# Mixer C's sample attention in pairs of sequences, squares summed by VectorE, and an unrolled layer loop, in a two-layer hybrid decoder step

## The reference

```
x = x + 1/2 * SwiGLU_1(rmsnorm(x))                 # 1024 -> 2048 -> 1024
h = rmsnorm(x);  z = h @ w_in                      # queries, keys, values, ... of three mixers
  A: dilated window attention, 3 groups of 4 heads # B: gated short convolution
  C: an indexer scores all keys, the best are kept, 8 query heads on 2 key/value heads attend to them
x = x + w_out( sum_i sigmoid(h @ w_gate)_i * (branch_i @ w_branch_i) )
x = x + 1/2 * SwiGLU_2(rmsnorm(x))
```

## Time and profile before

| what | us |
|---|---|
| median of three runs (lowest, highest) | 2748.9 (2746.89, 2760.05) |
| the profiled execution: its time, its span | 2747.25, 2745.7 |
| PE busy, share of the span | 2529.2 (92%) |
| DVE busy | 973.7 (35%) |
| ACT busy | 528.7 (19%) |
| POOL busy | 282.5 (10%) |
| DMA, mean over the span | 139 GB/s |

### The profile page before, as it was taken

The page is one execution under the profiler, slowest core; times in us unless marked ns, Lnnn a source line. Parts: engine busy times, 40 slices in busy tenths (PEclk is TensorE's granted clock), DMA queues, the critical chain, the costliest instruction groups (busy, mean ns, idle before and its releaser), DMA issues.

```text
span 2745.7 us, 33069 instructions
## 1 busy us (share of the span) xinstructions
PE 2529.2 (92%) x10482; PEld 1680.8 (61%) x10482; DVE 973.7 (35%) x1706; ACT 528.7 (19%) x1030; POOL 282.5 (10%) x532
## 2 busy tenths in 40 slices
PE   6997999998889899999989998999988898999998
PEld 4765567654447556667657664776544565676766
DVE  1001356754656542110010014667455664411000
ACT  2100221123221232111011003111323213311110
POOL 3430000000002120000243000000000102100000
PEclk9998999988999888999999999999899997789999
DMA  5475337373435341144446631573454443322342
GB/s 163 149 233 145 97 131 259 125 246 120 154 106 169 98 124 50 63 152 122 121 130 211 213 94 66 195 274 121 172 175 149 137 143 93 93 77 77 122 138 66
DMA packets 317953, 382.32 MB, mean 139 GB/s; under 512 B 23901, under 2 KB 300966, under 8 KB 316138
## 3 DMA queue, kind: packets, MB, share of 16 engines
q1 hardware_dynamic: 292290, 257.40, 30.3%
q0 software_dynamic: 19712, 118.79, 12.5%
q10 hardware_dynamic: 5800, 4.30, 0.5%
HBM read 374.80 MB, written 92.91 MB: 170 GB/s over the span
## 4 chain that ended last, share of the span: by engine, by line
PE 85%; DVE 5%; DMA 3%; issue 3%; ACT 3%; SPq 1%; DVEq 0%; ACTq 0%
PE ps L634 46%; PE ps L686 11%; PE ps L911 4%; PE ps L915 4%; PE ps L874 3%; PE ps L883 3%; PE ps L848 2%; PE ps L851 2%; PE ps L792 1%; DMA ring<-in_ffn_wd 1%; PE ps L901 1%; PE ps L728 1%; PE ps L823 1%; PE ps L738 1%; ACT pT L1024 1%
## 5 line engine op out<-in xcount | busy, mean ns | idle before, releaser
L634 PE MATMUL ps<-h,ring 128*128 128x320 f32 x3200 | 873.5, 436 | 21.5 <-DVE h L1300 17.8
L634 PEld LDWEIGHTS ps<-h,ring 128*128 128x128 f32 x3200 | 612.6, 192 | 279.0 <-DVE h L1300 11.4
L634 PE MATMUL ps<-area,ring 128*128 128x320 f32 x1280 | 355.1, 436 | 21.6 <-DMA ring<-in_ffn_wd 13.3
L686 PE MATMUL ps<-ring,h 128*128 128x256 f32 (+3 forms) x1440 | 321.3, 383 | 10.4 <-DVE h L1300 7.8
L634 PEld LDWEIGHTS ps<-area,ring 128*128 128x128 f32 x1280 | 244.4, 191 | 126.7 <-DMA ring<-in_ffn_wd 13.8
L686 PEld LDWEIGHTS ps<-ring,h 128*128 128x128 f32 (+1 forms) x1440 | 243.9, 178 | 82.8 <-issue 25.9
L1308 DVE TENSOR_TENSOR area<-silu,ps 128x320 f32 x64 | 31.2, 488 | 522.0 <-ACT silu L1049 522.0
L363 POOL DMA_DIRECT2D area<-in_cache_c_idx x256 | 137.0, 535 | 488.5 <-issue 473.6
L380 POOL DMA_DIRECT2D area<-in_cache_c_kv x176 | 98.5, 560 | 741.3 <-issue 741.3
L1024 ACT ACTIVATE kT<-ps 128x512 f32<-128x512 f32 (+3 forms) x248 | 125.9, 544 | 199.3 <-PE ps L851 118.8
L1315 DVE SCALAR_TENSOR_TENSOR x<-ps,x 128x320 f32<-128x320 f32 x48 | 23.6, 491 | 362.5 <-PE ps L634 362.5
(11 more groups left out here) (183 smaller groups left out, 2090.5 us busy)
## 6 DMA issues: line engine op xcount, KB each, us to landing
out_s_a_kv<-in_cache_a_kv POOLq DMA_DIRECT2D x64, 1020.0 KB, 9.1
ring<-in_w_in SPq DMA_DIRECT2D x80, 512.0 KB, 4.6
ring<-in_ffn_wg SPq DMA_DIRECT2D x64, 512.0 KB, 4.6
ring<-in_ffn_wu SPq DMA_DIRECT2D x64, 512.0 KB, 7.1
ring<-in_ffn_wd SPq DMA_DIRECT2D x64, 512.0 KB, 5.7
area<-in_cache_a_kv SPq DMA_DIRECT2D x32, 1024.0 KB, 6.5
ring<-in_w_gate SPq DMA_DIRECT2D x48, 512.0 KB, 4.5
area<-in_cache_c_kv POOLq DMA_DIRECT2D x176, 128.0 KB, 2.7
```

Of the source, the lines that this page charges most:

```text
L634: last = mm(bank(b, T), w[:, j, c0:c0 + P], rhs[:, j, :], start=(j == 0), stop=(j == k - 1))
L686: last = mm(dst, h3[:, k, t0:t0 + rows], w[:, k, :], start=(k == 0), stop=(k == KD - 1))
```

## The change

1. `sample_jobs` keeps kind "a" only. Mixer C gets functions of its own that take two sequences at a time, 4 pairs, with 64 score rows each, so all 128 PSUM partitions are used.
2. Keys are no longer turned by PE and copied by ACT: DVE turns the key half of a page buffer in place, in blocks of 32 x 32, in two instructions of 1024 columns per sequence. A score product then has 32 contraction rows and 32 output rows: one row quarter `q4` and one column group (sequence, kv head) of the array, 512 keys wide. There are 32 of them per pair, and their queries lie in `qR`, filled once per layer by 17 DVE copies (`c_queries`). The mask goes first, with four bf16 products of 512 columns and one of 64.
3. Maximum and exponential read PSUM directly (no DVE copy of the scores); the division by the sum moves behind the values, to a 128 x 128 piece. Probabilities are turned in 17 pieces of 128 x 128 for both sequences; values take 2 x 17 products with 64 output rows each, and the result is turned back by PE once per pair.
4. Four page buffers: the new one, with `kT`, `z`, `zt`, `y`, is the tensor `stage`. Sequences 0, 1 and 3 are loaded by POOL ahead of `chosenS`; 2, 4, 5, 6, 7 half by POOL and half by SP. 4 and 5 wait for the values of pair 0, 6 and 7 for those of pair 1.
5. The mean square: DVE adds the eight squares into the first one, PE makes one product per norm where it made eight.
6. `for l in range(DEPTH)` instead of the hardware loop, on all five engines; waits compare with constants.
7. Small memsets on DVE clear what the shared buffers have spoilt, since `stage`, `ab`, `uh`, `us`, `rot` now serve several purposes.

```diff
-SAMPLE_JOBS = 2 * NB
+SAMPLE_JOBS = NB
+PAIRS = NB // 2
-CBUFS = 3
+CBUFS = 4
+C_POOL = (16, 16, 8, 16, 8, 8, 8, 8)
+C_CHUNKS = ((0, 4), (4, 4), (8, 4), (12, 4), (16, 1))
...
-            with sp.Fori(0, DEPTH) as l:          (the same on every engine)
+            for l in range(DEPTH):
...
-                for b in range(CBUFS, NB):
-                    load_c_pages(sp, l, b, range(NPAGES // 2), c_in_sp)
+                sp.wait_ge(chosenS.sem, chosenS.at(l, 1))
+                alone(sp)
+                for b in (2, 4, 5, 6, 7):
+                    load_c_pages(sp, l, b, range(C_POOL[b], NPAGES), c_in_sp)
...
+                load_c_pages(pool, l, 0, range(NPAGES), c_in_pool)
+                load_c_pages(pool, l, 1, range(NPAGES), c_in_pool)
+                pool.wait_ge(k_out.sem, k_out.at(l, k_out.per_layer))
+                load_c_pages(pool, l, 3, range(NPAGES), c_in_pool)
                 pool.wait_ge(chosenS.sem, chosenS.at(l, 1))
+                for b in (2, 4, 5, 6, 7):
+                    load_c_pages(pool, l, b, range(C_POOL[b]), c_in_pool)
...
-            def mean_square(l, n, k):
-                pe.wait_ge(sq_ready.sem, sq_ready.at(l, (n - 1) * KD + k + 1))
-                ins = mm(bank(6, T), ones[:, :], squares[k], start=(k == 0), stop=(k == KD - 1))
+            def mean_square(l, n):
+                pe.wait_ge(sq_added.sem, sq_added.at(l, n * (KD - 1)))
+                mm(bank(6, T), ones[:, :], squares[0], start=True, stop=True).then_inc(ms_ready.sem, 1)
...
+                def c_scores(p):
+                    b0 = 2 * p
+                    pe.wait_ge(ck_turned.sem, ck_turned.at(l, b0 + 2))
+                    ...      # p == 0: wait for qR_ready; else: pe.wait_ge(cs_exp.sem, cs_exp.at(l, p))
+                    for q4 in range(4):
+                        mm(bank(q4), pick, hide, start=True, stop=False)
+                    mm(bank(4, NSAMP), pick, outS[:, PAST:KEYS], start=True, stop=False)
+                    for half in range(2):
+                        for s in range(2):
+                            for g in range(2):
+                                for q4 in range(4):
+                                    at, r0 = 2 * g + half, 64 * s + 32 * g
+                                    q = qR[q4 * 32:(q4 + 1) * 32, ((b0 + s) * 4 + at) * 32:((b0 + s) * 4 + at + 1) * 32]
+                                    k = cpages(b0 + s)[q4 * 32:(q4 + 1) * 32, :, at * 32:(at + 1) * 32]
+                                    mm(ps[r0:r0 + 32, q4 * 512:(q4 + 1) * 512], q, k, start=False, stop=(half == 1))
+                    ...      # four products with the 64 new keys
+                def c_turn(p, c):       # 4 (at last 1) transposes of 128 x 128 of probs into bank 5 + c % 2
+                def c_values(p, c):     # 8 (at last 2) products: 64 probabilities' columns x 128 values
+                def sample_c():
+                    c_scores(0); c_scores(1); c_out(0); c_out(1); c_back(1)
+                    c_scores(2); c_scores(3); c_out(2); c_out(3); c_back(3)
...
+                def sample_c():         # ACT, per pair p
+                        act.wait_ge(cs_max.sem, cs_max.at(l, p + 1))
+                        fn(probs ..., ps[:, 0:PAST] ..., ACT.Exp, ...)      # 128 x 2048
+                        fn(probs[:, PAST:KEYS], ps[:, PAST:KEYS], ACT.Exp, ...).then_inc(cs_exp.sem, 1)
+                        ...             # and a copy of each turned chunk
...
+                        if c >= 2:
+                            add_square(l, n + 1, c - 1)                     # DVE, in add_x
+                    add_square(l, n + 1, KD - 1)
...
+                def sample_c():         # DVE
+                    def keys_turn(b):
+                        ...             # waits for the pages of b
+                        for i in range(2):
+                            k = cpages(b)[:, 8 * i:8 * i + 8, 0:P]
+                            last = nc.vector.transpose(k, k)
+                    keys_turn(0); keys_turn(1); most(0); keys_turn(2); keys_turn(3); most(1); result(0); result(1)
+                    keys_turn(4); keys_turn(5); most(2); keys_turn(6); keys_turn(7); most(3); result(2); result(3)
```

More of the change, by code:

```diff
@@ L550, in _ @@
             pool.wait_ge(consts_in.sem, 48)
-            with pool.Fori(0, DEPTH) as l:
+            for l in range(DEPTH):
                 pool.wait_ge(x_ready.sem, x_ready.at(l, 1 - KD))
@@ L616, in _ @@
                 last.then_inc(turned_in.sem, 1)
-            for k in range(KD):
-                mean_square(0, 0, k)
-            with pe.Fori(0, DEPTH) as l:
+            mean_square(0, 0)
+            for l in range(DEPTH):
                 def arrived(q, i=0):
@@ L930, in sample_jobs @@
                     scores_of(0, 0)
-                    if kind == "a":
-                        with pe.Fori(0, NB // 2 - 1) as i:
-                            two(i)
-                    else:
-                        for i in range(NB // 2 - 1):
-                            two(i)
+                    with pe.Fori(0, NB // 2 - 1) as i:
+                        two(i)
                     scores_of(NB // 2 - 1, 1)
@@ new lines, in c_values @@
+                def c_values(p, c):
+                    n0, n_ = C_CHUNKS[c]
+                    pe.wait_ge(cs_pT.sem, cs_pT.at(l, p * len(C_CHUNKS) + c + 1))
+                    if c == 0 and p:
+                        pe.wait_ge(cs_done.sem, cs_done.at(l, p))
+                    for n in range(n0, n0 + n_):
+                        for s in range(2):
+                            v = cpages(2 * p + s)[:, n, P:256] if n < NPAGES else vc3[:, 2, :]
+                            last = mm(ps[64 * s:64 * s + 64, 7 * 512:7 * 512 + P], pTc[:, n * P + 64 * s:n * P + 64 * s + 64], v,
+                                      start=(n == 0), stop=(n == NPAGES))
+                    if c == len(C_CHUNKS) - 1:
+                        last.then_inc(cs_out.sem, 1)
@@ new lines, in c_back, with c_out @@
+                def c_back(p):
+                    pe.wait_ge(cs_rows.sem, cs_rows.at(l, p + 1))
+                    tr(bank(7, P, at=256), rowsC, ident).then_inc(cs_back.sem, 1)
+                def c_out(p):
+                    for c in range(len(C_CHUNKS) + 1):
+                        if c < len(C_CHUNKS):
+                            c_turn(p, c)
+                        if c == 1 and p % 2:
+                            c_back(p - 1)
+                        if c >= 1:
+                            c_values(p, c - 1)
@@ L1035, in _ @@
             squares_of_x(0, 0)
-            with act.Fori(0, DEPTH) as l:
+            for l in range(DEPTH):
                 def norm(n):
@@ L1423, in conv @@
                 def conv():
+                    step(nc.vector.memset(uh3[:, :, 0:2], 0.0))
                     for c in range(4):
@@ L1590, in _ @@
                 ffn(0)
+                for t in (z3, zt3, y3):
+                    last = nc.vector.memset(t[64:P, 2, :], 0.0)
+                step(last)
                 norm(1)
```

366 lines of the change are left out of this document (207 added, 159 removed).

## The result

The changed kernel takes 2580.9 us, the median of 4 runs (2574.6 to 2599.4), where the kernel before took 2754.5 us on the same chip: a ratio of 0.938, interval 0.932 to 0.944. The profiled execution went from 2747.25 to 2583.66 us, 163.6 us less.

What follows compares the result with a forecast made beforehand. PE was taken as the bound, with 85% of the chain, partly at its lower clock. Savings of 87.6 (sample stage), 15 (norms) and 6 (loop), 108.6 us, from 2747.25 gave 2639 us, range 2597 to 2710.

Steps and rivals of the forecast that it cites:

- The loop: Layer boundary: PE's 6.05 us with nothing to wait for disappears in straight code; 6 us saved once, 0 at worst.
- The sample stage: Mixer C's samples, summed step by step: 109.5 us against 152.3 and 154.3, saving 87.6 us over two layers.
- First keys: Start of mixer C's samples: DVE turns keys of sequences 0 and 1 while PE has nothing to do, 5.0 us.
- values of a pair: Mixer C's samples: 17 transposes and 34 products, half an overlap of the column halves at the high clock, 9.2 us.
- pages: Mixer C's samples: page loads of sequences 4 to 7, from end of pair 0's values to last page, 42.2 us.
- The 32 score products: Mixer C's samples, per pair: 4.5 us, between 8.0 with only row quarters overlapping and 2.0 with all 16 tiles.
- The new wait: Second half of mixer C's samples: PE waits for page issues, idle 15 us or more behind pair 1's values.
- The norms: Six norms: fewer mean-square products on PE, less DVE's last addition, net 2.7 us each; 15 us saved in all.
- Costs at nothing: Query copies (5 to 6 us on DVE), sequence 3's pages and small memsets hide in other waits, adding no time.
- A: Mixer C's samples: only row quarters overlap, scores 12 us instead of 4.5, values in a row; 2706 us, chance 0.20.
- B: Mixer C's samples: score products don't overlap, 32 us per pair, slower than before; 2862 us, chance 0.06.
- C: Mixer C's samples: full overlap, higher clock, page issues 1.1 us each; 19 us less per layer, 2601 us, chance 0.12.

Runs made afterwards that it cites:

- the filling: Changed kernel with each pair's values directly behind its scores, plus nine and seven idle TensorE products in two waits around the prompt attention: 2555.7 us, ratio 0.928.

## Why the prediction was wrong, point by point

*The step that failed: "The loop. ... 6 us, once; below it would be 0".* The loop was taken as one jump. The boundary gave its 6.1 us, but the written-out loop is worth 41 in the profile and 48 by the medians. I set no bound from above, and so the range had no room for it. Of the 55 us that the forecast missed (163.6 measured, 108.6 forecast) 35 are the loop and some 20 the sample stage; with the loop as forecast the time would have lain inside the range. Some 20 of the other 35 us of the loop are the projection and the prompt attention, by the clock (2 of them the shorter waits there). What is left lies in mixer A's samples (5.2), the first FFN (3.9), the merge of C (2.6), the index scores (2.1) and the FFNs' first halves (2.2), less 1.7 in C's stage. Of the first FFN's part 3.3 is a shorter wait for weights in layer one, 10.0 us where the kernel before had 13.3, and with VectorE's loop alone the same wait took 19.6, so it is hardly the loop. In the merge of C, the index scores and the FFNs' first halves PE is again busy for less time at the lower level (4.9, 2.9 and 3.9 us less, which saves half of that). What stays open is why the clock falls less often in straight code. That the register compares of five engines make each signal a little later may be a reason, but no run takes it apart, and after the clock and the weights it would be left with mixer A's samples for the most part: single engines gave 17 and 5 us, and SP, POOL and ACT were not tried alone.

*The sample stage, 109.5 us forecast, 98.0 and 101.4 measured.* It saved 107.2 us over both layers where 87.6 were forecast. The layout of the chain was right piece by piece, and every term was somewhat too large. First keys 4.5 (5.0), scores with mask 6.4 (7.5), maximum 2.4 (2.6), scores of the last pair 5.4 (7.5), values of a pair 7.2 (9.2), pages 40.8 (42.2), the last two values 16.2 (19.4). The transpose, which no row had shown, came out at 1.20 against 1.22. The products were the mis-sized term, those of the values most of all: 34 of them took 4.4 us for a pair (the four groups of L976 above) where I had put 6.5, half an overlap of the two column halves. They overlap in full, as the timeline of PE shows in pair 1, where the products of both sequences start together:

```profile
943.24 0.27 PE L976 MATMUL ps<-area,ab 128*64 128x128 f32 x1
943.24 0.27 PE L976 MATMUL ps<-stage,ab 128*64 128x128 f32 x1
```

The 32 score products I put at 4.5, between row quarters alone and full overlap; they too overlap in full, and take 4.0 us because they run at the low clock (0.50 from 911.3 to 915.2), and 3.2 in the last pair of layer one (0.63).

*The new wait* came as described: PE stands behind the values of pair 1 and again ahead of pair 3's scores, some 13 us each time where I had said 15 or more for the first, and the releaser is DVE, itself waiting for pages. The experiment with half of the issues shows it as the bound.

*The merge of C* was not in the sum: PE comes out of the new stage at the high clock, and with the loop's part (2.6) this gives 6 us over both layers.

*The norms*: 15 forecast, 14.4 in the norm stages. The first FFN of layer one hides its part behind a wait for weights, as said.

*Costs at nothing*: the query copies, the pages of sequence 3 and the memsets did not show; the merge ahead takes 96.0 us with DVE 67.7 busy.

*Rivals.* A and B fall: tile order makes no difference and 32 products take 4.0 us, not 12 or 32. C, at a chance of 0.12, had the right overlap and issue period (1.15 us). Its other half, a higher clock in the stage, did not come (0.73 and 0.70 against 0.78 and 0.76); the clock rose in stages that I had not looked at. The rows were there: a window of 20.6 us at 0.51 in the prompt attention of the kernel before.

## What to carry to other kernels

Before pricing a change by its own stage, list the stretches in which the engine that bounds the kernel runs at its lower clock, and what it waited for ahead of each: a change that touches only the waits there can move time that you are not counting (here 16 idle products per layer gave 12 to 15 us). Give every "costs nothing" or "once" a bound from above too. When a stage waits for many small transfers, halve the issues and halve the bytes in two separate kernels: it takes two runs to see which of them is the bound.

## What the runs showed of the hardware

- One stage of 300 records (314 with the filling) took 62.6 to 78.9 us in different kernels, as its mean granted clock went from 1.00 to 0.68; 16 useless products per layer in two waits of about 2 us gave 12 to 15 us by the medians.
- A wait of the same length did not always bring the clock down: behind 1.46 us the next 10 us ran at 0.72 in one layer and at 1.00 in the other.
- Thirty-two products of 32 x 32 tiles and 512 columns took 2.28 us at the high clock, little more than two products of 512 columns take alone (1.00 us each); at the low clock they took 4.0 us, and 4.1 in another order.
- A page issue with its register load took 1.15 us on POOL whether 128 KB or half of it followed, and 1.07 us on ScalarE's queue. Half as many issues made the stage 15.1 and 18.5 us shorter, half the bytes 0.3 and 0.6.
